# Tap matrices in another place and loaded earlier, phase rotations ahead of the state products, column products split in two, gathers a pair sooner

## What is computed

```python
def body(h, u_blk):          # S5: 64 groups of 16 channels, 64 complex states each
    bu = jnp.einsum('blgc,gpc->blgp', u_blk.astype(jnp.complex64), b_bar)
    bu = bu.at[:, 0].add(lam_bar * h)
    a = jnp.broadcast_to(lam_bar, bu.shape)
    _, hs = lax.associative_scan(_linear_combine, (a, bu), axis=1)
    y = jnp.real(jnp.einsum('blgp,gcp->blgc', hs, c_c)) + d_g * u_blk
    return hs[:, -1], y
...
ag = jax.nn.gelu(y).astype(x.dtype) @ w['w_glu'][o]
mix = ag[..., :D_MODEL] * jax.nn.sigmoid(ag[..., D_MODEL:])
...
hg = jnp.einsum('nd,edf->nef', x, w_gate[sl])      # experts, eight at a time
hu = jnp.einsum('nd,edf->nef', x, w_up[sl])
act = (jax.nn.silu(hg.astype(f32)) * hu.astype(f32)) * combine[:, sl, None]
y = y + jnp.einsum('nef,efd->nd', act.astype(x.dtype), w_down[sl]).astype(f32)
```

## Time and profile before

| | us |
|---|---|
| median of 3 runs | 1083.25 |
| lowest and highest of them | 1079.65, 1083.58 |
| the profiled execution | 1082.61 |
| its span, first to last instruction | 1080.8 |
| TensorE matmul busy in it | 940.0 (87%) |
| VectorE, ScalarE, GpSimd busy | 416.9, 196.8, 377.5 |

### The profile page before, as it was taken

How to read it: one execution, slowest core, us unless ns; L and a number is a source line. 1 busy time by engine, 2 the same in 40 slices (tenths; PEclk the granted TensorE clock), 3 DMA queues, 4 the chain that set the end, 5 groups by cost and what they waited for, 6 DMA issues and landing times.

```text
span 1080.8 us, 15965 instructions
## 1 busy us (share of the span) xinstructions
PE 940.0 (87%) x5748; PEld 571.2 (53%) x5748; DVE 416.9 (39%) x921; ACT 196.8 (18%) x386; POOL 377.5 (35%) x647
## 2 busy tenths in 40 slices
PE   4999989899978887787887499999989999788786
PEld 3888879454644444343444376444555555444442
DVE  4500355786542222322246851132464233121226
ACT  4413322222200000000045231002441000000003
POOL 1378900382366676666532820000021211101100
PEclk9999999999889999999998799999979999999998
DMA  7127932450799999999982935622066999999965
GB/s 256 45 73 278 351 148 76 184 204 24 280 388 386 414 428 421 420 384 405 398 337 71 128 118 210 257 87 89 20 233 274 418 421 425 424 423 426 421 268 201
DMA packets 45921, 292.29 MB, mean 270 GB/s; under 512 B 10737, under 2 KB 12017, under 8 KB 26391
## 3 DMA queue, kind: packets, MB, share of 16 engines
q1 hardware_dynamic: 35463, 270.18, 63.3%
q0 software_dynamic: 8640, 16.03, 4.0%
q10 hardware_dynamic: 1760, 5.31, 1.6%
HBM read 270.36 MB, written 36.80 MB: 284 GB/s over the span
## 4 chain that ended last, share of the span: by engine, by line
PE 54%; DMA 31%; DVE 5%; issue 3%; SPq 3%; POOL 2%; ACT 1%; POOLq 0%; DVEq 0%; ACTq 0%
DMA arena<-in_w_gu 17%; PE ps L747 13%; PE ps L890 9%; PE ps L1034 8%; DMA arena<-in_w_down 7%; PE ps L1239 5%; PE ps L1024 4%; PE ps L961 2%; DMA arena<-scratch_hd,idx_now 2%; PE ps L1197 2%; PE ps L1193 2%; DMA arena<-scratch_kp 2%; PE ps L920 2%; POOL arena L2404 2%; SPq L574 1%
## 5 line engine op out<-in xcount | busy, mean ns | idle before, releaser
L1034 PE MATMUL ps<-arena 128*64 128x256 f32 x2048 | 235.6, 385 | 48.0 <-DMA arena<-in_w_gu 47.8
L1034 PEld LDWEIGHTS ps<-arena 128*64 128x64 f32 x2048 | 146.8, 138 | 137.2 <-DMA arena<-in_w_gu 45.2
L2305 POOL TENSOR_TENSOR arena<-arena 128x32 f32<-128x32 f32 (+5 forms) x232 | 117.9, 508 | 163.8 <-DMA arena<-in_s_d 67.6
L2404 POOL TENSOR_TENSOR arena<-arena 128x256 f32<-128x256 f32 (+3 forms) x192 | 132.3, 689 | 41.7 <-POOL arena L2404 41.4
L747 PE MATMUL ps<-arena 128*128 128x256 f32 (+1 forms) x640 | 142.1, 383 | 0.3 <-ACT arena L1351 0.3
L1024 PE MATMUL ps<-arena 128*64 128x512 f32 x512 | 126.0, 636 | 13.3 <-DMA arena<-in_w_down 12.8
L747 PEld LDWEIGHTS ps<-arena 128*128 128x128 f32 x640 | 121.0, 190 | 19.1 <-ACT arena L1351 0.5
L890 PE MATMUL ps<-arena 128*128 128x512 f32 x256 | 116.2, 605 | 1.0 <-DMA arena<-in_w_out 0.8
L2048 DVE TENSOR_TENSOR arena<-arena,ps 128x128 f32<-128x128 f32 x64 | 18.3, 287 | 247.6 <-ACT arena L1494 247.5
L1494 ACT ACTIVATE arena<-ps 128x128 f32<-128x128 f32 x64 | 17.7, 277 | 469.4 <-PE ps L1034 469.4
L1024 PEld LDWEIGHTS ps<-arena 128*64 128x64 f32 x512 | 38.0, 145 | 79.6 <-issue 68.8
(11 more groups left out here) (225 smaller groups left out, 986.5 us busy)
## 6 DMA issues: line engine op xcount, KB each, us to landing
arena<-in_w_gu SPq DMA_DIRECT2D x64, 2048.0 KB, 13.2
arena<-in_w_down SPq DMA_DIRECT2D x64, 1024.0 KB, 14.3
arena<-in_w_in SPq DMA_DIRECT2D x10, 1024.0 KB, 6.7
scratch_yd<-arena SPq DMA_DIRECT2D x2, 4160.0 KB, 17.7
arena<-scratch_yd SPq DMA_DIRECT2D x16, 512.0 KB, 7.3
arena<-in_w_out SPq DMA_DIRECT2D x1, 4096.0 KB, 12.3
scratch_hd<-arena ACTq DMA_DIRECT2D x8, 512.0 KB
arena<-in_w_glu SPq DMA_DIRECT2D x2, 2048.0 KB, 7.4
```

Of the source, the lines that this page charges most:

```text
L1034: mm = pe.matmul(ps[CAP * f:CAP * f + CAP, 2 + s, 0:256], XT[l][:, kc, CAP * s:CAP * s + CAP], WGU[l][i][s][:, kc, 256 * f:256 * f + 256], ...
L2305: step(g_.tensor_tensor(out, a, b, op))
L2404: g_.tensor_tensor(o, x, y, f).then_inc(sem("matrix_steps"), 1)
```

## The change

Five edits in one:

1. **Places.** `TT`, one region until now, becomes two: half 0 at arena offset 14336, half 1 at 28832. The phases and column buffer of half 1 (`HALF_AT[1]`) goes from 14336 to 24736. Weights of `glu`, two regions of expert weights of layer 1 and the rows fetched at its end change places to fit (`WGL_HALVES`, `WGU`, `YG`; not shown).
2. **Loads.** SyncE issues the taps 0 to 3 of half 0 as soon as `scratch_kp` is written, then at `zs 3` full the phases `turns_in_1` (until now loaded behind `turns_in_0`) and the taps 4 to 7.
3. **VectorE and GpSimd.** `rotated(4)` to `rotated(7)` go ahead of `states(0)`, `add_turned(4)` to `(7)` ahead of `last_states(0)`.
4. **TensorE.** For blocks 0 to 3 all input products come first (`from_inputs`), when the taps are there, without a wait for the states; only the first product in each bank opens it (`start`). The state products (`from_states`) follow, then `turned(0)` and `turned(1)`. Blocks 4 to 7 go pair by pair as before. PSUM jobs and ScalarE's copies follow this order.
5. **Gathers.** `gather(2)` is issued right after `gather(1)`, ahead of the first build, and the loop has scatter(p-1), gather(p+2), build(p).

```diff
-    j += [(("zs", 7), "dve"), (("y", 0), "act"), (("y", 1), "act")]
-    for q in range(2, 8):
-        j += [(("y", q), "act" if q < 4 else "dve"), (("yT", q - 2), "act")]
+    j += [(("zs", 7), "dve")] + [(("y", q), "act") for q in range(4)] + [(("yT", 0), "act"), (("yT", 1), "act")]
+    for q in range(4, 8):
+        j += [(("y", q), "dve"), (("yT", q - 2), "act")]
...
-        HALF_AT = [A + 10240, A + 14336]
+        HALF_AT = [A + 10240, A + 24736]
...
-        TT = place(A + 24736, 2, 2 * 4, L * KQ)
+        TT = [place(at, 2 * 4, L * KQ) for at in (A + 14336, A + 28832)]
...
-            for half in range(2):
-                if half:
-                    sp.wait_ge(sem("combined_0"), 4)
-                load(TURNS[:, half, 0:2].rearrange("p m r k -> p (m r k)"),
-                     T["turns"].rearrange("p (h n) -> h p n", h=2)[half], f"turns_in_{half}")
+
+            def load_turns(half):
+                load(TURNS[half], T["turns"].rearrange("p (h n) -> h p n", h=2)[half], f"turns_in_{half}")
+            load_turns(0)
...
             sp.wait_ge(sem("taps_out"), 16)
+            sp.wait_ge(sem("h_2"), 5)
+            for s in range(L // 2):
+                taps(sp, s, 0)
             ring.wait_full(sp, "zs", 3)
-            for s in range(L):
+            load_turns(1)
+            for s in range(L // 2, L):
                 taps(sp, s, 0)
             ring.wait_full(sp, "zs", 7)
...
-            def columns(q):
-                ring.wait_free(pe, "y", q)
-                if q % 4 == 0:
-                    pe.wait_ge(sem(f"taps_in_{q // 4}"), 16 * L)
-                    pe.wait_ge(sem("ends_ready"), 1)
+            def outs_of(pr):
+                return [slot("y", pr // 4)[0:SC, b, pr % 4 * P:(pr % 4 + 1) * P] for b in range(2)]
+
+            def from_inputs(pr, start=True):
+                for b, out in enumerate(outs_of(pr)):
+                    pe.matmul(out, U[:, 2 * pr + b, NS:UC], taps_of_group(pr, b), start=start, stop=False,
+                              skip_group_check=True)
+
+            def from_states(pr):
+                for h_, g_ in ((HR, GR), (HI, GI)):
+                    for b, out in enumerate(outs_of(pr)):
+                        half = slice(64 * b, 64 * b + 64)
+                        mm = pe.matmul(out, h_[half, pr], g_[half, pr, 1:L + 1], start=False, stop=h_ is HI,
+                                       skip_group_check=True)
+                return mm
+
+            def wait_states(q):
                 if q in (0, 4, 6):
                     pe.wait_ge(sem("states_in"), (1, 3, 4)[q // 3])
-                o = slot("y", q)
-                for j in range(4):
-                    pr = 4 * q + j
-                    outs = [o[0:SC, b, j * P:(j + 1) * P] for b in range(2)]
-                    for b in range(2):
-                        pe.matmul(outs[b], U[:, 2 * pr + b, NS:UC], taps_of_group(pr, b), start=True, stop=False)
-                    for h_, g_ in ((HR, GR), (HI, GI)):
-                        for b in range(2):
-                            half = slice(64 * b, 64 * b + 64)
-                            mm = pe.matmul(outs[b], h_[half, pr], g_[half, pr, 1:L + 1], start=False, stop=h_ is HI)
-                full(mm)
+                if q == 0:
+                    pe.wait_ge(sem("ends_ready"), 1)
...
-            columns(0)
-            for q in range(1, 8):
-                columns(q)
-                if q >= 2:
-                    turned(q - 2)
+            pe.wait_ge(sem("taps_in_0"), 16 * L)
+            for q in range(4):
+                ring.wait_free(pe, "y", q)
+                for j in range(4):
+                    from_inputs(4 * q + j, start=j == 0)
+            for q in range(4):
+                wait_states(q)
+                for j in range(4):
+                    mm = from_states(4 * q + j)
+                full(mm)
+            turned(0)
+            turned(1)
+            pe.wait_ge(sem("taps_in_1"), 16 * L)
+            for q in range(4, 8):
+                ring.wait_free(pe, "y", q)
+                wait_states(q)
+                for j in range(4):
+                    from_inputs(4 * q + j)
+                    mm = from_states(4 * q + j)
+                full(mm)
+                turned(q - 2)
             turned(6)
...
                 y_out(q)
-                if q >= 2:
-                    gelu(q - 2)
-            for kc in range(2, KC):
+            for kc in range(KC):
                 gelu(kc)
...
             scanned(0)
+            dve.wait_ge(sem("turns_in_1"), 16)
+            for q in range(4, 8):
+                rotated(q)
             ring.wait_full(dve, "u", 7)
             states(0, 0, PAIRS // 2)
             dve.sem_inc(sem("states_in"), 1)
-            dve.wait_ge(sem("turns_in_1"), 16)
-            for q in range(4, 8):
-                rotated(q)
             scanned(1)
...
                     gather(1, 1)
+                    gather(2, 0)
                     pool.wait_ge(sem(f"lists_{l}"), 3 * r + 3)
...
-                    with pool.Fori(0, EP // 2 - 1) as k:
+                    with pool.Fori(0, EP // 2 - 2) as k:
                         for p, half in ((2 * k + 1, 1), (2 * k + 2, 0)):
-                            gather(p + 1, 1 - half)
                             scatter(p - 1, 1 - half)
+                            gather(p + 2, half)
                             build(p, half)
+                    scatter(EP - 4, 0)
+                    gather(EP - 1, 1)
+                    build(EP - 3, 1)
+                    scatter(EP - 3, 1)
+                    build(EP - 2, 0)
...
             first_states()
-            last_states(0)
             for q in range(4, 8):
                 add_turned(q)
+            last_states(0)
             last_states(1)
```

32 lines of the change are left out of this document (18 added, 14 removed).

## The result

The changed kernel takes 1075.76 us (median of 6 executions, 1072.88 to 1082.86), the kernel before 1083.41 (6 executions beside them, 1079.24 to 1085.2). The ratio is 0.9939 with a 95% interval of 0.991 to 0.9968, so 6.6 us faster, between 3.5 and 9.8. Forecast were 1078.0 and a range of 1074.0 to 1082.5. The profiled execution of the changed kernel took 1072.88 us, the fastest of the six; the one of before, 1082.61, is an ordinary one. At the start of `glu` the changed kernel is 10.07 us ahead (652.89 against 662.96), and 0.4 us are lost again behind it. Of the 10.07 us, 1.3 were there when the write of `scratch_kp` landed (590.14 against 591.46), 3.9 are the start of the first input product counted from that landing, and 4.85 the column stage.

What follows compares the result with a forecast made beforehand. TensorE was taken to bound the column stage, whose start the taps set, and DMA the experts of layer 0. Gains of 4.05 and 0.6, together 4.65 us, off 1082.61 gave 1078.0 us, range 1074.0 to 1082.5.

Steps and rivals of the forecast that it cites:

- rival B: Column stage and layer 0 experts: tail only 0.5 us, no new dry stretch, more from gathers; 1075.5 us, chance 0.18.
- Taps and phases in SyncE's queue: Loads before the column stage: first four taps issued near 591.9, last landing at 614.4, 4.05 us sooner (2.5 to 5.0).
- The 1.5 us of start: SyncE's tap read: 1.5 us of start before the first four taps, then 2.13 us each, through at 601.9.
- the bounds of the tail: End of the tap read: between 0.5 and 3.0 us beyond the last taps' transfer, 1.5 taken.
- Phases just in time: VectorE before the rotations: phases land at 604.4, wanted at 604.9; states ready 15.0 us after the phases, 6.6 us early.
- the stage keeps its 44.5 us: TensorE's column stage: input products about 12 us, state products 9.5 us; length unchanged, ending at 658.9.
- Gathers: Experts of layer 0: 1.7 us won at pair 2, 1.1 lost at pair 0; net 0.6 us (-1.0 to 3.0).
- the dry stretch: Layer 0 experts, 324 to 330 us: DMA at 262 and 337 GB/s; its removal worth 1.7 us.
- rival C: Experts of layer 0: builds become the bound, margin 1.2 us a pair; 1092.6 us at 1 us uncovered, chance 0.09.
- One opening per bank, places: Flag of 24 TensorE products and new addresses: no cost, 0 us; flag bounded by 0 to one instruction's duration.
- Rival A: Last four taps share DMA engines with ScalarE's: 10.7 us instead of 8.5, landing 616.6, time 1080.2, chance 0.15.
- D: SyncE's queue: taps don't come sooner, only changing places with the phases; gain 0.5 us, time 1081.5, chance 0.08.

Runs made afterwards that it cites:

- ScalarE's wait: Changed kernel, but ScalarE issues its four taps of half 1 only when all eight of half 0 have landed: 1074.7 us, ratio 0.9926.
- kernel with mixed blocks: Changed kernel with input and state products of blocks 0 to 3 again pair by pair, other engines as changed: 1086.9 us, ratio 1.0041.
- early taps with the gathers: Changed kernel with ScalarE's wait, but blocks 0 to 3 mixed and the old order on VectorE and GpSimd: 1079.6 us, ratio 0.9963.
- kernel with all blocks split: Changed kernel with blocks 4 to 7 split too, each block's input products ahead of its state products: 1070.5 us, ratio 0.9886.
- kernel of late taps: Changed kernel with SyncE's first four taps issued behind the fourth driven block instead of behind the norm: 1092.4 us, ratio 1.0095.

## Why the prediction came out as it did

The time fell into the range, 2.2 us below the forecast, just outside the forecast's own 1076 to 1080 and next to rival B's 1075.5. One term of about 4 us was missing from the sum, and the wide range took it in; to that extent the hit is luck. Step by step:

- *Taps and phases in SyncE's queue, 4.05 us sooner (2.5 to 5.0).* Right in mechanism and size: 3.7 us less wait in the profiles, 4.0 us by the ratio of the kernel that has this part and the gathers with ScalarE's wait. Counted from the landing of `scratch_kp`, the first four taps were there after 10.8 us (forecast 10.4), the phases after 13.8 (12.9), the last tap after 23.0 (22.9). 2.1 us a tap held in every kernel while no second queue ran beside it. The 1.5 us of start and the bounds of the tail stand on no row; what the trace shows is a first landing 4.4 us after its issue, 2.3 more than the pace of a tap.
- *Phases just in time.* Right: 0.72 us of wait. The cover, however, is smaller than I wrote. The states are ready 15.4 us after the phases (603.97 to 619.40), as worked out, and in the kernel with mixed blocks TensorE did wait 7.3 us for them.
- *TensorE: "the stage keeps its 44.5 us".* This is the step that failed. I priced the split state products at "some 0.6 with the overlap" a group, from rows in which they alternate with input products, and even named a loss there as the thing to watch. Alone they take 0.45 to 0.48 us a group and the input products 0.44 to 0.46. So the input products took 9.5 us and not 12, the state products 7.2 and not 9.5. The split is worth 4.5 us in blocks 0 to 3 (41.9 against 37.4 us without the cost of the halved clock, the same in two pairs of profiles). The other 0.3 of the 4.85 us is the clock, which came back after 4.9 us of the stage instead of 5.9.
- *Gathers, 0.6 us (-1.0 to 3.0).* Nothing against it: 0.3 to 0.6 by the mean length of the stage, inside its spread. The new waits came as worked out, 2.95 us for pair 0, and the dry stretch moved rather than went. (A pair is 264/16 = 16.5 us, not 16.4, which makes rival C's margin 1.3 us.)
- *One opening per bank, places: 0.* Pairs that open a bank and pairs that do not start 0.44 us apart alike. Neither was tried by itself.
- *Sum.* By the ratios, early taps with the gathers are 4.0 us, the split 4.0, and 1.4 go back for the wait of ScalarE's taps that the changed kernel lacks: 6.6 us. These are steps of one chain of kernels, so that they add up proves nothing; each ratio is known to 1.6 to 3.1 us only. The 4.0 for the split agrees with the 4.5 of the profiles.
- *Rival A* is real in kind: two queues served together halve each other's rate when they write the same partitions. Whether it strikes depends on when ScalarE's turn comes; in the profiled execution of the changed kernel that was late enough to cost nothing, in that of the kernel with all blocks split it cost 6 us of wait (17.2 against 11.2), where A had priced it at 2.2. *B* predicted the time best, 1075.5, but for reasons that were not at work: a shorter tail and more from the gathers. *C*: no sign of it in twelve executions. *D*: the gain is there.

## What to carry to other kernels

- Price a regrouping of matmuls from rows in which the same kind runs alone. Where products of two shapes alternate, ask what each costs by itself; here grouping them by shape gave 0.23 to 0.28 us for each pair of channel groups (12 matrix instructions).
- A reorder on one engine may be free only because another edit hides it. Ask of each part what it costs without the others: the rotations first cost 7.3 us of wait where the blocks were mixed.
- A second engine's DMAs behind a critical load are not behind it. If the later load can wait, make it wait for the landing; if it can't, let it write to partitions 64 apart, which here raised the joint rate to 1.6 times that of one tap once both queues were served together.

## What the runs showed of the hardware

- *When a second queue gets its turn.* ScalarE's taps of half 1 were first served 5.4 to 9.6 us after their issue in the six kernels without ScalarE's wait, and 1.9 to 4.8 us where less of SyncE's queue was left, behind some of SyncE's transfers but not all; from then on the two queues shared evenly. In the other direction SyncE's phases, issued at 596.8, were served from 602.9 on, during the last of ScalarE's four taps. The Trainium skill, DMA: Bandwidth & Descriptors, section on queues, rings and completion order, says that each DMA engine goes round-robin between the queues that have work. By that rule ScalarE's taps would have been served from the issue on; the 8.7 us in the changed kernel speak against it for the first stretch, the equal shares of 53.9 and 53.2% in the kernel of late taps for it afterwards. What sets the length of the first stretch stays open: at ScalarE's issue, in the kernel before four of SyncE's taps were served alone first (landings 605.7 to 613.1) and two after it, in that of late taps two and the phases first and four after it.
- *Sharing between two DMA queues* gained nothing where both wrote the same half of the partitions, 107 to 136 GB/s together (windows from 614 us on), and about 1.6 times one tap's rate where one wrote partitions 0 to 63, the other 64 to 127, and both were served together, 191 to 208. One tap alone moves 119 to 131 (2.0 to 2.2 us for 256 KB). In one queue the order of partitions makes no difference.
- *TensorE:* the instructions of the 64-row state products start 0.06 us apart alone (7.15 us for 128) and 0.07 in groups of 8 between input products; the input products of a pair fall from 0.59 to between 0.44 and 0.46 us.
